# Expert weights loaded two units at a time into double slots of a six-unit buffer

## What is computed

```
def swiglu(h, w_gate, w_up, w_down):
    a = jnp.einsum('bsd,df->bsf', h, w_gate)
    b = jnp.einsum('bsd,df->bsf', h, w_up)
    return jnp.einsum('bsf,fd->bsd', jax.nn.silu(a) * b, w_down)

def moe_swiglu(h, router, w_gate, w_up, w_down):
    ...
    for e in range(N_EXPERTS):
        y = y + combine[..., e:e + 1].astype(h.dtype) * swiglu(h, w_gate[e], w_up[e], w_down[e])
    return y
```

## Time and profile before

| | us |
|---|---|
| median of 3 runs | 1361.1 (1360.14 to 1362.15) |
| the profiled execution's own time | 1362.48 |
| its span, first to last instruction | 1360.7 |
| PE busy in the span | 1338.6 (98%) |
| DVE busy | 1130.1 (83%) |
| ACT busy | 966.0 (71%) |
| experts' loads, `raw<-in_moe_up`, `_gate` and `_down` | 336 of 1024 KB |

### The profile page before, as it was taken

How to read it: one execution, slowest core, us unless ns; L and a number is a source line. 1 busy time by engine, 2 the same in 40 slices (tenths; PEclk the granted TensorE clock), 3 DMA queues, 4 the chain that set the end, 5 groups by cost and what they waited for, 6 DMA issues and landing times.

```text
span 1360.7 us, 18862 instructions
## 1 busy us (share of the span) xinstructions
PE 1338.6 (98%) x6489; PEld 1068.8 (79%) x6489; DVE 1130.1 (83%) x998; ACT 966.0 (71%) x904; POOL 13.7 (1%) x26
## 2 busy tenths in 40 slices
PE   9999999999999999999999999999999999999997
PEld 7877888888787787777777777777777778777775
DVE  6576544444655789999999999999999999999998
ACT  6554533333454478888888888888888887888886
POOL 1100000000000000000000000000000000000000
PEclk9999999999999999999999999999999999999999
DMA  9813555555351049999999999999999999999994
GB/s 377 315 69 118 209 188 188 191 188 194 130 218 61 18 190 413 421 422 422 422 409 359 419 422 421 423 421 371 405 422 422 422 422 396 385 421 422 421 423 178
DMA packets 61401, 433.26 MB, mean 318 GB/s; under 512 B 7066, under 2 KB 7241, under 8 KB 10032
## 3 DMA queue, kind: packets, MB, share of 16 engines
q1 hardware_dynamic: 59312, 426.80, 77.6%
q0 software_dynamic: 1888, 5.78, 1.3%
q10 hardware_dynamic: 160, 0.14, 0.0%
HBM read 431.60 MB, written 1.09 MB: 318 GB/s over the span
## 4 chain that ended last, share of the span: by engine, by line
PE 89%; DVE 5%; DMA 2%; issue 2%; ACT 2%; DVEq 0%; ACTq 0%; SPq 0%
PE ps L1478 19%; PE ps L1479 19%; PE ps L1480 19%; PE ps L1874 6%; PE ps L1873 6%; PE ps L1888 3%; PE ps L1889 3%; DVE wlo L921 3%; PE ps L1919 2%; DMA raw<-in_moe_down 1%; PE ps L1807 1%; PE ps L1576 1%; PE ps L1603 1%; PE ps L1485 1%; PE ps L1915 1%
## 5 line engine op out<-in xcount | busy, mean ns | idle before, releaser
L921 DVE TENSOR_TENSOR wlo<-raw,whi 128x2048 fp32r<-128x2048 f32 (+1 forms) x403 | 908.9, 2283 | 101.9 <-PE ps L1480 63.8
L548 ACT ACTIVATE whi<-raw 128x2048 fp32r<-128x2048 f32 (+1 forms) x403 | 765.3, 1915 | 118.9 <-PE ps L1480 44.2
L1478 PE MATMUL ps<-whi,xhi 128*128 128x512 f32 (+1 forms) x880 | 346.6, 394 | 6.1 <-DVE wlo L921 2.6
L1479 PE MATMUL ps<-wlo,xhi 128*128 128x512 f32 (+1 forms) x880 | 342.2, 389 | 0.0
L1480 PE MATMUL ps<-whi,xlo 128*128 128x512 f32 (+1 forms) x880 | 342.0, 389 | 0.0
L1478 PEld LDWEIGHTS ps<-whi,xhi 128*128 128x128 f32 x880 | 165.2, 188 | 45.7 <-DVE wlo L921 7.3
L1480 PEld LDWEIGHTS ps<-whi,xlo 128*128 128x128 f32 x880 | 165.2, 188 | 34.3
L1479 PEld LDWEIGHTS ps<-wlo,xhi 128*128 128x128 f32 x880 | 165.3, 188 | 32.4
L1874 PE MATMUL ps<-wlo,xhi 128*64 128x512 f32 x392 | 155.2, 396 | 0.0
L1873 PE MATMUL ps<-whi,xhi 128*128 128x512 f32 x392 | 153.6, 392 | 0.0
L1478 PE MATMUL ps<-whi,thi 128*128 128x512 f32 x320 | 127.1, 397 | 0.1
(11 more groups left out here) (251 smaller groups left out, 1078.1 us busy)
## 6 DMA issues: line engine op xcount, KB each, us to landing
raw<-in_moe_up SPq DMA_DIRECT2D x112, 1024.0 KB, 9.3
raw<-in_moe_gate SPq DMA_DIRECT2D x112, 1024.0 KB, 9.8
raw<-in_moe_down SPq DMA_DIRECT2D x112, 1024.0 KB, 9.6
raw<-in_ffn_up SPq DMA_DIRECT2D x14, 1024.0 KB, 4.8
raw<-in_ffn_gate SPq DMA_DIRECT2D x14, 1024.0 KB, 4.8
raw<-in_ffn_down SPq DMA_DIRECT2D x14, 1024.0 KB, 4.8
raw<-in_dil_w_in SPq DMA_DIRECT2D x10, 1024.0 KB, 4.7
raw<-in_swa_w_in SPq DMA_DIRECT2D x4, 1024.0 KB, 19.5
```

Source lines behind the costliest of these rows:

```text
L548: act.activation(whi[:, c % HIS, 0:span(c)], raw[:, c % RAW, 0:span(c)], ACT.Copy).then_inc(hi_ready, 1)
L921: dve.tensor_tensor(wlo[:, c % LOS, 0:n], raw[:, c % RAW, 0:n], whi[:, c % HIS, 0:n].bitcast(F32), ALU.subtract).then_inc(lo_ready, 1)
L1478: pe.matmul(dst, ahi, bhi, start=start, stop=False)
L1479: pe.matmul(dst, ahi, blo, start=False, stop=False)
```

## The change

The expert tensors are laid out in HBM so that two successive units lie together: a row of 16 KB per partition, the first unit's 8 KB and then the second's. One DMA then brings both units into two neighbouring slots of `raw`. The buffer is no larger, so it is now three double slots. The attention weights and the dense layer's keep their loads of one unit.

```
-            def load_two(c, rounds, w, first_unit):
-
-                for i in range(2):
-                    load(c + i, rounds, w[:, bass.ds(first_unit + i, 1), :])
+            def load_two(c, rounds, w, pair_of_units):
+
+
+                sp.wait_ge(lo_ready, c + 1 + RAW * rounds - RAW + 1)
+                dst = raw[:, c % RAW:c % RAW + 2, :].rearrange("p k f -> p (k f)").rearrange("p (k f) -> p k f", k=1)
+                sp.dma_start(dst, w[:, bass.ds(pair_of_units, 1), :]).then_inc(raw_full[c % RAW], 16)
...
                     for g in range(2):
-                        load_two(MOE0 - 4 + 4 * g, r + 2 * s, moe_in[g], a + 2 * s)
-                        load_two(MOE0 - 2 + 4 * g, r + 2 * s, moe_in[g], b + 2 * s)
-                    load_two(MOE0 + 4, r + 2 * s, moe_out, a + 2 * s - 2)
-                    load_two(MOE0 + 6, r + 2 * s, moe_out, b + 2 * s - 2)
+                        load_two(MOE0 - 4 + 4 * g, r + 2 * s, moe_in[g], a + s)
+                        load_two(MOE0 - 2 + 4 * g, r + 2 * s, moe_in[g], b + s)
+                    load_two(MOE0 + 4, r + 2 * s, moe_out, a + s - 1)
+                    load_two(MOE0 + 6, r + 2 * s, moe_out, b + s - 1)
...
             def cut(c, rounds):
 
-                act.wait_ge(raw_full[c % RAW], 16 * uses(c, rounds))
+                landed = c - c % 2 if c >= MOE0 - 4 and not isinstance(rounds, int) or c >= MOE0 else c
+                act.wait_ge(raw_full[landed % RAW], 16 * uses(landed, rounds))
...
+    for name in ("moe_gate", "moe_up", "moe_down"):
+        w = arrays[name].reshape(-1, 2, P, UNIT).transpose(0, 2, 1, 3)
+        arrays[name] = np.ascontiguousarray(w).reshape(-1, P, 2 * UNIT)
```

More of the change, by code:

```diff
@@ L448, in _, with load_in @@
             load_chunks(C_DI, len(CHUNKS))
-            def load_in(c, rounds, first_unit):
-                for i in range(4):
-                    load(c + i, rounds, moe_in[i // 2][:, bass.ds(first_unit + i % 2, 1), :])
-            def load_two(c, rounds, w, first_unit):
-                for i in range(2):
-                    load(c + i, rounds, w[:, bass.ds(first_unit + i, 1), :])
+            def load_two(c, rounds, w, pair_of_units):
+                sp.wait_ge(lo_ready, c + 1 + RAW * rounds - RAW + 1)
+                dst = raw[:, c % RAW:c % RAW + 2, :].rearrange("p k f -> p (k f)").rearrange("p (k f) -> p k f", k=1)
+                sp.dma_start(dst, w[:, bass.ds(pair_of_units, 1), :]).then_inc(raw_full[c % RAW], 16)
+            def load_in(c, rounds, step):
+                for g in range(2):
+                    load_two(c + 2 * g, rounds, moe_in[g], step)
             def load_steps(pair, a, b):
@@ L464, in load_steps @@
                     for g in range(2):
-                        load_two(MOE0 - 4 + 4 * g, r + 2 * s, moe_in[g], a + 2 * s)
-                        load_two(MOE0 - 2 + 4 * g, r + 2 * s, moe_in[g], b + 2 * s)
-                    load_two(MOE0 + 4, r + 2 * s, moe_out, a + 2 * s - 2)
-                    load_two(MOE0 + 6, r + 2 * s, moe_out, b + 2 * s - 2)
-                load_two(MOE0 + PAIR_UNITS - 4, r, moe_out, a + 2 * STEPS - 2)
-                load_two(MOE0 + PAIR_UNITS - 2, r, moe_out, b + 2 * STEPS - 2)
+                        load_two(MOE0 - 4 + 4 * g, r + 2 * s, moe_in[g], a + s)
+                        load_two(MOE0 - 2 + 4 * g, r + 2 * s, moe_in[g], b + s)
+                    load_two(MOE0 + 4, r + 2 * s, moe_out, a + s - 1)
+                    load_two(MOE0 + 6, r + 2 * s, moe_out, b + s - 1)
+                load_two(MOE0 + PAIR_UNITS - 4, r, moe_out, a + STEPS - 1)
+                load_two(MOE0 + PAIR_UNITS - 2, r, moe_out, b + STEPS - 1)
             load_in(MOE0, 0, 0)
@@ L474, in _ @@
             small = sp.value_load(jobs_i[0:1, 3:4], min_val=0, max_val=NE - 1)
-            load_steps(0, 0, 2 * STEPS * small)
+            load_steps(0, 0, STEPS * small)
             sp.wait_ge(pairs_ready, 1)
@@ L480, in _ @@
                 small = sp.value_load(jobs_i[0:1, bass.ds(2 * pair + 3, 1)], min_val=0, max_val=NE - 1)
-                load_in(MOE0, ROUNDS * pair, 2 * STEPS * large)
-                load_steps(pair, 2 * STEPS * large, 2 * STEPS * small)
+                load_in(MOE0, ROUNDS * pair, STEPS * large)
+                load_steps(pair, STEPS * large, STEPS * small)
             for t in range(TILES):
```

## The result

The changed kernel took **1454.28 us** (median of 4 runs, 1452.2 to 1460.34) beside 1361.62 us for the kernel before (4 runs, 1360.14 to 1366.09): a ratio of 1.0684, 95% interval 1.0667 to 1.0701. It is slower by 92.7 us. The forecast was 1365.3, with 1371 as the upper end: the sign was right and the size wrong by more than twenty times. The profiled execution has a span of 1450.4 us, 89.7 more than before.

A forecast was written before the change was run, and what follows sets the result against it. PE was taken to bound the kernel before (29.25 us per step), loads 2% behind; after the change, the buffer loop (29.66). Steps +2.9, changes of pair +0.9, end +0.4: +4.2 us, from 1361.1 to 1365.3, range 1358 to 1371.

The forecast's parts named there:

- From issue to landing: Joined load of two units, from SP's issue to its landing in the buffer: 7.2 us, bounds 7.0 and 7.3.
- the loop: Way through the three double slots, DVE's cuts, issue, landing, ACT's start: 29.66 us per step, longer than PE's 29.25.
- I take 4.90 us: Stream of expert loads: one double in 16 KB rows every 4.90 us, between 4.97 and 4.81.
- DVE's part: DVE in a step: 5.60 us from d0's first cut to d1's, then 4.82 to the end of d1's second cut.
- ACT's start: From a double's landing to DVE's first cut of it, with ACT's wake, cut of 1.92 and hand over: 2.05 us.
- SP's 0.19: SP, from the end of DVE's cut to the issue of the next load: 0.19 us.
- ACT at nothing: ACT's small operations between a double's two cuts fit in its 4.9 us, so they cost nothing.
- The first pair, the changes of pair and the end: Outside the regular steps: first pair 178.5 us, three changes of pair +0.3 each (+0.9), the very end +0.4.
- The rivals: Four cases for the changed kernel's time: 1365.3 us (chance 0.34), 1368.8 (0.2), 1359.9 (0.24), 1357.4 (0.14).
- or 30 and more, which would mean another loop, through PE and ACT: Sign of a wrong forecast in the next profile: `fold` 30 us or more apart, through a loop taken as free.
- The second rival: Loop through the buffer binds and 16 KB rows move no faster, 29.88 us per step: 1368.8 us, chance 0.2.
- Slack before: Kernel before: a unit needed 4.8 us on an empty queue but was given 10.1, over 5 us of cover.

The follow-up runs named there:

- the stream: Kernel of expert loads alone, whole computation left out, issue timing varied; fed 2 MB loads in 16 KB rows landed 4.894 us apart.
- the table: Loads alone, 16 KB rows, two outstanding, ACT operation between landing and next issue lengthened by phase: landings 4.895 us apart at 0.02 us lateness, 5.855 at 3.93.
- both cuts shorter: Changed kernel with DVE's cuts of both units of each expert double on 1024 of 2048 columns: 1368.78 us, ratio 1.0063 to the kernel before.
- one shorter: Changed kernel with DVE's cut of only the second unit of each expert double on 1024 of 2048 columns: 1395.07 us, ratio 1.0227 to the kernel before.

## Why the prediction was wrong

The failed step is this one: "From issue to landing. ... A double needs 1 MB more, 2.4: 7.2 us. ... A double issued later than 7.2 us before its turn to land lands late." As a latency on an empty queue 7.2 was only a little short (2 MB on one took 7.4 to 7.8 in the runs of loads alone, over the upper bound of 7.3). What I made of it was wrong. A stream of loads is not kept up by issuing each within its latency. The limit measured is a lateness of 1.0 to 1.4 us with 4.89 us per double, thus an issue 8.4 to 8.8 us before the turn to land (2 x 4.89 less the lateness), and beyond it the rate itself falls, which the loop had no term for. I took the rate as a constant 4.90 and the cover as the only thing at stake.

- *"I take 4.90 us"* per double: right as a property of the rows (4.894 in the stream, 4.9 in the kernel with short cuts), not reached in the changed kernel, where a double took 5.5 us on average in the stretch read.
- *DVE's part*, 5.60 + 4.82, ACT's start and the cut, SP's 0.19: right. From landing to the end of DVE's cuts the changed kernel has 6.6 to 7.2 us, which is 2.05 + 2.20 + 2.28 with 0 to 0.7 for the small operation between; the issue follows 0.03 or 0.18 later.
- *The loop, 29.66 us per step*: with 8.6 in place of 7.2 it is 31.06, still under the 32.9 measured. The rest is the falling rate. Two relations give it: lateness is the way from landing to issue, some 7.1 us, less the pitch of the landings; and the pitch follows from lateness by the table. At 4.90 lateness would be 2.2, which the table doesn't allow at 4.90; the two meet at 1.6 us and 5.5. Six doubles at 5.5 are 33.0 us. With both cuts shorter the way is 5.65, and 0.75 gives 4.90. With one shorter it is about 6.0, and they meet near 1.0 and 5.0, which is 30.0 us for a step where 31.0 were measured: the doubles there are in part over the knee and in part under it, and averages don't carry that.
- *"ACT at nothing"* and fewer issues worth nothing: right; ACT's cuts start with the landings and their small operations fit between.
- *The first pair, the changes of pair and the end*, +0.9 and 0.4 of the sum: measured +2.9 for the changes, +2.0 before the first `fold` and +1.8 at the end. All small and all forecast too low. In the run with both cuts shorter all three are gone (first `fold` at 516.85, changes of 37.96 to 38.10, end 21.7), which speaks for the same cause but doesn't show it, as DVE's own work is shorter there too.
- *The rivals*: none had a stream that slows down when it is fed late. The sentence on what would show it wrong named it only from outside: "or 30 and more, which would mean another loop, through PE and ACT". It was 30 and more, but through the same loop that I had drawn. The second rival, "because the runs of 16 KB are moved no faster", is refuted by the stream (431 against 423 GB/s).
- *Slack before*: "over 5 us of cover. The change uses it up". So it is, and the runs add what the forecast lacked: either half of it can be taken for 0.7%, and with both the queue tips.

There was a row that could have warned: the earlier trace rows shows 4.8 us for 1 MB on an empty queue and 2.48 us pitch in a full one. The 2.3 us between them are a start and an end that a fed queue hides. As I read it now, they are only hidden if the load ahead still has that much left on every one of the 16 engines, not on average.

## What to carry to other kernels

Joining two loads into one DMA halves the count of loads that a buffer can hold in flight; before doing it, work out how much of the load ahead is still to come at each issue, and leave at least 4 us of it at this rate, more than the latency of one load would ask for (7.6 less 4.9 is 2.7). That figure was measured with loads of 2 MB; for loads of 1 MB the runs show only that 2.5 us ahead are too few (405 GB/s against 423). Two waits that are each harmless can be ruinous together when they share one margin, so add them up before costing either at nothing. And a DMA share shown as 9 tenths or more doesn't mean that the queue is fed: read GB/s beside it, and the distance of the landings.

## What the runs showed of the hardware

- The rate of a stream of 2 MB loads with two outstanding is flat at 428 to 429 GB/s up to 1.0 us of lateness, and falls to 394 at 1.4 and 361 at 3.9. Half of the fall comes between 1.0 and 1.4 us. The first and the last of the 16 engines finish a load 0.7 to 0.8 us apart before the fall, and 1.9 to 2.5 us apart at 1.4 to 2.0 us of lateness.
- The first packet of a 2 MB load in rows of 16 KB takes 0.75 to 1.95 us on an empty queue, mostly over 1.0, where others take 0.61, and is mostly long too on an engine that comes to it under 2 us after the issue (125 of 144 such packets in the changed kernel took over 0.7 us). It counts as busy; so a starved queue shows as packets that take longer (60 of the 90 us here), and less as idle time. What the engine does in that time the trace doesn't show.
- Rows of 16 KB move 2 MB in 4.894 us and rows of 8 KB in 4.97, 1.5% apart, if the queue is fed. This kernel, whose PE needs 29.25 us per step, could have taken at most 5.7 us from it.
